# Reordered opening of a fused encoder layer: units 2 and 3 of the first matrix ahead of the second quarter of the rows

## What is computed

```python
mod = jax.nn.silu(c) @ w_ada[l] + b_ada[l]
sh1, sc1, g1, sh2, sc2, g2, sh3, sc3, g3 = jnp.split(mod, N_MOD, axis=-1)
h = modulate(rms_norm(x, ffn1_norm[l]), sh1, sc1)
x = x + 0.5 * g1[:, None, :] * swiglu(h, ffn1_w1[l], ffn1_w3[l], ffn1_w2[l])
```

## Time and profile before

| | us |
|---|---|
| median of 3 executions | 1025.04 |
| lowest, highest | 1024.93, 1028.9 |
| the profiled execution | 1029.99 |
| its span | 1028.3 |
| TensorE busy in the span | 998.1 |
| VectorE busy | 750.3 |
| ScalarE busy | 505.0 |
| GpSimd busy | 229.0 |

### The profile page before, as it was taken

The page is one execution under the profiler, slowest core; times in us unless marked ns, Lnnn a source line. Parts: engine busy times, 40 slices in busy tenths (PEclk is TensorE's granted clock), DMA queues, the critical chain, the costliest instruction groups (busy, mean ns, idle before and its releaser), DMA issues.

```text
span 1028.3 us, 18555 instructions
## 1 busy us (share of the span) xinstructions
PE 998.1 (97%) x6946; PEld 868.3 (84%) x6946; DVE 750.3 (73%) x1039; ACT 505.0 (49%) x691; POOL 229.0 (22%) x191
## 2 busy tenths in 40 slices
PE   7999999999999999999999989999999999999997
PEld 5779999999888787777677667878999999988887
DVE  6777878877788768678899994567778787783334
ACT  5555444444323234687878953465434344433221
POOL 0024454452123210101000000202435354200100
PEclk9999999999999999999999999999999999999999
DMA  9557667765787826421121301235576767653322
GB/s 355 203 177 200 164 196 201 182 188 167 256 290 269 321 86 241 143 83 62 47 79 45 96 27 63 82 115 154 151 175 184 188 175 206 197 173 100 103 82 83
DMA packets 63190, 162.21 MB, mean 158 GB/s; under 512 B 5440, under 2 KB 7760, under 8 KB 63008
## 3 DMA queue, kind: packets, MB, share of 16 engines
q1 hardware_dynamic: 44720, 110.79, 30.5%
q0 software_dynamic: 18416, 50.68, 20.6%
HBM read 159.36 MB, written 2.10 MB: 157 GB/s over the span
## 4 chain that ended last, share of the span: by engine, by line
PE 77%; issue 8%; DVE 7%; ACT 3%; DMA 3%; POOL 1%; SPq 1%; DVEq 0%; POOLq 0%; ACTq 0%
PE psum L1884 13%; PE psum L1886 13%; PE psum L1885 13%; PE psum L1956 10%; PE psum L1958 10%; PE psum L1957 10%; DMA raw<-wu 1%; DMA sraw_a<-ws 1%; DMA raw<-ws 1%; DVE dif L1643 1%; PE psum L2185 1%; DVE wlo L1353 1%; PE psum L2187 1%; PE psum L2186 1%; PE psum L2214 1%
## 5 line engine op out<-in xcount | busy, mean ns | idle before, releaser
L580 ACT ACTIVATE whi<-raw 128x1024 fp32r<-128x1024 f32 x92 | 97.3, 1057 | 227.2 <-PE psum L1886 209.1
L1102 DVE TENSOR_TENSOR wlo<-raw,whi 128x1024 fp32r<-128x1024 f32 x94 | 118.5, 1260 | 120.2 <-ACT whi L580 119.7
L1886 PE MATMUL psum<-ghi,wlo 128*128 128x512 f32 (+2 forms) x384 | 143.7, 374 | 0.0
L1885 PE MATMUL psum<-glo,whi 128*128 128x512 f32 (+2 forms) x384 | 143.4, 373 | 0.0
L1884 PE MATMUL psum<-ghi,whi 128*128 128x512 f32 (+2 forms) x384 | 143.0, 372 | 0.0
L1884 PE MATMUL psum<-hhi,whi 128*128 128x512 f32 x320 | 130.7, 408 | 3.0 <-DVE wlo L1102 1.3
L1886 PE MATMUL psum<-hhi,wlo 128*128 128x512 f32 x320 | 125.0, 391 | 0.0
L1885 PE MATMUL psum<-hlo,whi 128*128 128x512 f32 x320 | 124.9, 390 | 0.0
L1956 PE MATMUL psum<-forms,whi 128*128 128x256 f32 x432 | 121.1, 280 | 0.0
L1957 PE MATMUL psum<-forms,whi 128*128 128x256 f32 x432 | 120.5, 279 | 0.0
L1958 PE MATMUL psum<-forms,wlo 128*128 128x256 f32 x432 | 120.5, 279 | 0.0
(11 more groups left out here) (266 smaller groups left out, 2347.1 us busy)
## 6 DMA issues: line engine op xcount, KB each, us to landing
raw<-wu SPq DMA_DIRECT2D x96, 512.0 KB, 3.4
ada<-wada POOLq DMA_DIRECT2D x56, 512.0 KB, 5.3
sraw_a<-ws SPq DMA_DIRECT2D x36, 512.0 KB, 6.2
raw<-ws SPq DMA_DIRECT2D x36, 512.0 KB, 6.5
sraw_b<-ws SPq DMA_DIRECT2D x36, 256.0 KB, 4.3
sraw_a<-ws POOLq DMA_DIRECT2D x18, 512.0 KB, 6.0
raw<-ws POOLq DMA_DIRECT2D x18, 512.0 KB, 6.0
early<-wada SPq DMA_DIRECT2D x16, 512.0 KB, 15.2
```

The lines of the kernel that those rows point to most:

```text
L580: nc.scalar.activation(whi[:, slot, :], raw[:, slot, :], ACT.Copy).then_inc(hi_done, 1)
L1102: nc.vector.tensor_tensor(wlo[:, slot, :], raw[:, slot, :], whi[:, slot, :], ALU.subtract).then_inc(lo_done, 1)
L1885: nc.tensor.matmul(dst, a, rlo, start=False, stop=False)
L1886: return nc.tensor.matmul(dst, b, rhi, start=False, stop=stop)
```

## The change

No instruction is added or removed but for `keep_busy`: two and four of its matmuls go, and fifteen come behind the first block sums. On SyncE's queue units 2 and 3 move in front of the four pieces of q = 1. On ScalarE the root goes ahead of the first copy of rows, the table load ahead of the high parts of units 0 and 1, the high parts of units 2 and 3 ahead of the first two h copies, and the copies of rows 1 and 2 move back. On VectorE the reciprocal goes ahead of the small values, whose last ten (now `bound_values`) move behind block 3; the low parts of the four units are placed among and behind the work of block 0. On TensorE products of k = 0, 1 of units 0 to 2 go ahead of most of block 1's rows, and blocks 1 and 2 are spread among products.

```diff
@@ SyncE
-                if q < 2:
-                    for u in range(2):
-                        sp_.dma_start((raw, raw2)[q][:, u, :], wu[2 * q + u]
-                                      ).then_inc((raw_loaded, extra_loaded)[q][u], 16)
+                if q == 0:
+                    for u in range(4):
+                        sp_.dma_start((raw, raw2)[u // 2][:, u % 2, :], wu[u]
+                                      ).then_inc((raw_loaded, extra_loaded)[u // 2][u % 2], 16)
@@ ScalarE
             act.wait_ge(ones_set, 2)
+            root(0)
             rows_copy(0)
-            root(0)
+            nc.scalar.preload_act_table(ACT.Silu)
             hi(0, 0)
             hi(0, 1)
-            nc.scalar.preload_act_table(ACT.Silu)
-            rows_copy(1)
             first_h(0)
             first_h(1)
+            hi_extra(0)
+            hi_extra(1)
             h_copy(0, 0)
             h_copy(0, 1)
-            hi_extra(0)
-            hi_extra(1)
+            rows_copy(1)
             first_h(2)
             first_h(3)
-            rows_copy(2)
             h_copy(0, 2)
             h_copy(0, 3)
+            rows_copy(2)
@@ VectorE
                 step(nc.vector.tensor_scalar(half_gain, vec("hg_norm"), 0.5, None, ALU.mult))
+
+            def bound_values():
+
                 step(nc.vector.tensor_tensor(t8, lb_e[:, 0:8], lb_e[:, 8:16], ALU.add))
...
             add_first_squares(1)
+            rms_inverse(0, rms_done, rinv_done)
             small_values()
-            rms_inverse(0, rms_done, rinv_done)
-            lo(0, 0)
-            lo(0, 1)
             rows_add(0)
             for q in range(BLOCKS):
                 block_columns(q)
...
                 first_tmp(2 * q)
                 first_tmp(2 * q + 1)
+                if q == 0:
+                    lo(0, 0)
                 first_lower(2 * q)
                 if q == 0:
+                    lo(0, 1)
+                first_lower(2 * q + 1)
+                if q == 0:
+                    lower_extra(0)
+                    lower_extra(1)
                     rows_add(1)
-                first_lower(2 * q + 1)
                 if q == 1:
                     rows_add(2)
-                if q in (0, 1):
-                    lower_extra(q)
                 if q == 2:
                     late_rows()
+            bound_values()
             ffn_up(0)
@@ TensorE
             block_rows(0, 0)
-            keep_busy(7, 2)
             norm_rb(0)
             block_rows(0, 1)
             keep_busy(3, 3)
             block_sums(0)
+            keep_busy(3, 15)
+            for k in range(2):
+                first_unit(0, range(k, k + 1))
+                first_unit(1, range(k, k + 1))
             block_rows(1, 0)
+            first_unit(2, range(0, 2))
             block_rows(1, 1)
-            keep_busy(3, 4)
-            first_unit(0, range(0, 1))
+            first_unit(3, range(0, 1))
             block_sums(1)
-            first_unit(0, range(1, 2))
-            first_unit(1, range(0, 2))
+            first_unit(3, range(1, 2))
             block_rows(2, 0)
-            block_rows(2, 1)
-            first_unit(2, range(0, 2))
-            block_sums(2)
             first_unit(0, range(2, 4))
             first_unit(1, range(2, 4))
-            first_unit(3, range(0, 2))
+            block_rows(2, 1)
             first_unit(2, range(2, 4))
+            block_sums(2)
             first_unit(3, range(2, 4))
```

## The result

| | before | changed |
|---|---|---|
| median of 6 executions | 1025.56 us | 1035.88 us |
| lowest, highest | 1024.93, 1028.9 | 1033.75, 1036.77 |
| the profiled execution | 1029.99 | 1033.75 |
| its span | 1028.3 | 1032.1 |

The account below looks back on a forecast made before the run. The opening was taken as bound by TensorE, then by VectorE's tail behind late third sums: +5.55 us of delay less 1.8 of slack gave +3.8 on the median 1025.04, so 1028.8 us, range 1025.0 to 1032.5.

Parts of the forecast that it names:

- cover behind the third sums: TensorE steps between block 2's sums and k = 6: 18 before, 10 after; 5.6 us less against 1.8 us of slack.
- VectorE's tail: VectorE's own work from the start of block 2's sums to k = 6's lower part: 11.75 us, left unchanged.
- The head: Opening up to block 0's sums: root and reciprocal ready at about 14.8, sums at about 18.1, 2.6 us earlier.
- the sign of being wrong: Listed in the prediction: third sums before 36.5, no hole before k = 6, or a half clock between 20 and 58.
- Case C: Opening: not slower, because third sums come early and VectorE's tail isn't the bound; best -2.0 us, 1023.0; chance 0.13.
- Step 5: TensorE's order from 23.7 through blocks 1 and 2: hole of 1.3 us before k = 2, block 2's sums at 39.7.
- Step 6: End of the opening: holes of 1.5 and 2.4 us, k = 6 ready at 51.4, last round ending at 57.0, +3.7 to +3.8.
- the 11.75 us: Time from the start of block 2's sums to k = 6's lower part, all VectorE's own work, taken as unchanged.
- Rival B: Last round: the clock falls behind the 2.4 us hole, costing 1.6 us; +5.4 in all, 1030.4; chance 0.27.
- Step 2: Low parts 0 and 1 behind the rows: block 0's sums 2.6 us earlier, and 1.6 us of half clock doesn't come back.
- Step 3: Fifteen fillers behind block 0's sums at 0.31 us each: 4.7 us, from 19.0 to 23.7, covering VectorE's work.
- D: Behind the opening: the delay is given back later, at a TensorE wait or transfer; 0 to +2 us, 1026; chance 0.10.

Follow-up runs that it names:

- e1: The changed kernel with TensorE's list of before, all else as changed; ratio 1.0017 to before (+1.7 us).
- e3: The changed kernel with block 2's second rows ahead of the k = 2, 3 steps and its sums behind three of them; ratio 1.0040 (+4.1 us).
- g2: The changed kernel with block 3's four long VectorE products over half their columns, for the time alone; ratio 1.0044 (+4.5 us).
- g1: The changed kernel with SyncE's transfer order of before, the rest as changed; ratio 1.0079 (+8.1 us).
- f1: The changed kernel again, no edit, for a second trace and more times; ratio 1.0096 (+9.8 us).
- h1: The changed kernel once more, no edit, for a third trace and more times; ratio 1.0089 (+9.1 us).
- f2: The kernel before again, no edit, for a second trace; ratio 0.9992 (-0.8 us).
- g3: The changed kernel without the fifteen fillers behind block 0's sums; ratio 1.0092 (+9.4 us).
- e2: The changed kernel with 5 filler calls before the round of k = 4, 5 and 7 before that of k = 6, 7; ratio 1.0062 (+6.4 us).
- h2: The kernel before with 31 filler calls on TensorE ahead of the round of k = 4, 5, nothing else changed; ratio 1.0090 (+9.2 us).
- e4: The kernel before with 23 filler calls on TensorE ahead of the round of k = 4, 5, nothing else changed; ratio 1.0056 (+5.7 us).

## Why the prediction was wrong

**Right.** The bound and the path: cover behind the third sums shrinks from 18 steps to 10, VectorE's tail becomes the bound, and the last round starts late (e1, e3 and g2 each show it). Holes of 1.13, 1.78 and 2.24 us stood where 1.3, 1.5 and 2.4 were forecast. The head came as said, with a root at 14.65 and sums at 18.50, some 0.4 us late, as was the start of the norm sums (13.61, 13.20 before). Transfers are hidden (g1). The bound values run from 53.35 to 55.25 and VectorE then waits 2.28 us: hidden. Clock 1.00 from 20 to 26: held; the sign of being wrong that the prediction named, a half clock between 20 and 58, came in the last round. Case C failed: third sums before 36.5 would have shown it, they came at 40.66.

**Mis-sized in the opening: +3.8 forecast, +7.0 measured.** By the ledger:
- Step 5, "the sums of block 2 start at 39.7": 40.66, +0.96. I had put this in a bound, "if semaphores add 0.1 us at each of eight handovers", and the trace shows that for a good part: a change between kinds of matmul takes some 0.1 us beyond 0.234 a product. The product that follows the rows at 27.80 takes 0.34 to the next start, and from the last product before them (26.49) to the rows it is 0.31. Seven such changes stand outside the holes, 0.65 us. From the second sums to k = 2 it is 3.98 us instead of 3.75, and low part 1 was not "just met": 0.3 us were lost at 24.47. Less the 0.27 us by which the first product came earlier (23.43, forecast 23.7), these make 0.9 of the 0.96.
- Step 6, "51.4": with the sums at 40.66 the 11.75 us give 52.4, the round starts at 52.92, +0.56. From the third columns to block 3's columns it is 8.38 us, 8.02 in the earlier trace rows: VectorE stands still for 0.40 us ahead of the tmp at 42.40, as in the traces of e1, e3, f1, g1, g2 and h1, and as before and f2 do not; its cause stays open. And 0.2 us lie between the end of the lower part and the product.
- Rival B happened: +1.77. I gave it 0.27; it was there in all four traces of this TensorE list with its fillers, and in g3. The earlier trace rows spoke against it, with a hole of the same length and no fall at once, but I had not read what stood ahead of that hole. In the trace of before it is this window:

```profile
560.00:587.50 27.50, 27.50 (x348) 21.12 (x346) 25.50 (x46) 26.88 (x39) 0.00 (x0) 1.00 0.19 59
```

27.5 us of TensorE without a gap. Here two holes within 18 us stood ahead of the third. The Trainium skill ("TensorE: Matmul & The Clock Gate", "What's actually happening") says that the gate follows the recent activity of the array; the trace agrees, 1.00 behind the first and second hole, 0.57 behind the third, and 1.00 throughout in e2, where fillers took up most of the last two. Why the second hole left 1.00 and the third did not is not shown by itself.

3.74 + 0.96 + 0.56 + 1.77 = 7.03 us, the whole of the opening. The last term is 1.66 by the starts, and the 0.1 us then belongs to the start of the last round in before.

**Two steps were wrong and did no harm.** Step 2 counted 1.6 us of half clock before as won. There was nothing to win: in before TensorE waits for a piece of block 2 (this is its weight load), and only then goes on to the third sums, whatever was lost ahead:

```profile
31.66 0.14 PEld L2102 LDWEIGHTS psum<-early,cs 128*32 128x32 f32 x4 [0.75 <-DMA early<-wada]
```

f2 lost twice as much and was no later. The forecast of the third sums was built from the new order's own steps, so the error did not enter the sum. Step 3 priced a filler at 0.31 us: thirty records took from 19.42 to 23.01, 0.24 us for each of fifteen. TensorE then waited for the first lower part of h until 23.43, so the first product came where it was expected (23.7).

**The steps that failed.** Two did. The first is the opening's sum, short by 3.3 us through the terms above, half of it the clock that the forecast left out as rival B. The second is "The opening's rows are no cause of that gap that I can see, so I add the difference to the median", one to one, and D, which allowed only that a delay is given back. h2 shows the opposite: 7.1 to 7.3 us of pure lateness cost 9.2 (7.9 to 10.6). The table shows how uneven it is: openings up to 55.9 cost -1.0 to +1.7 us, 56.1 costs 4.1 and 4.6, 59 costs 4.5 to 6.4, and 60.8 to 63.6 costs 8.1 to 9.8, with g3, the latest, at one to one. "Everything behind the opening is released by TensorE's own steps" fails in the first grouped stage: in h2's trace TensorE waits there for low parts whose chain comes from transfers of 8.36 and 7.62 us. The earlier trace rows already had 3% of the chain on transfers. With the opening right (+7.0) and one to one the forecast would have been 1032.0, inside the range; with h2's price it is 1034.2 and more. It took both errors to leave the range.

## What to carry to other kernels

Before moving an operation that feeds a long chain on another engine, count the steps that stand behind it, not those ahead: here eight steps fewer behind the third sums ended the slack of 1.8 us, and every us after that was paid in full, the clock on top. To price a delay far from the end of a kernel, shift the unchanged kernel by that much with idle fillers and time it; the price may be over one to one. And don't compare two single profiled executions end to end, since a difference of some us can lie in a stage that the change doesn't touch.

## What the runs showed of the hardware that was not expected

- A delay early on can cost more than itself: 7.1 to 7.3 us cost 9.2 (h2), in a kernel otherwise unchanged, and the extra arose between 61 and 145 us of its trace. 5.0 us cost 5.7 (e4), and 9.5 us cost 9.4 (g3).
- Two holes of nearly the same length, 2.24 and 2.19 us, with different ends: the clock fell to 0.57 to 0.61 behind the first (the changed kernel's three traces and g1) and not behind the second (e3). The changed kernel had holes of 1.13 and 1.78 us in the 18 us ahead of it, e3 one of 0.28 us. And the same list can go either way: behind the hole of 1.25 us at 20 the clock was 0.51 in before, behind 1.26 us in e4 it was 1.00.
- A half clock of 6.7 us cost nothing where before waits for a transfer later on anyway (f2), and 4 us of it cost 1.6 in a stretch that TensorE bounds (changed against e2).
- Fillers in a row take 0.23 to 0.24 us each (fifteen in 3.59 us, the 31 of h2 in 7.08), not the 0.31 us that three of them suggest.
- TensorE loses about 0.1 us at each change from one kind of matmul to another, 0.65 us over the seven that count here.
